# Row stores before a weight load, sums moved in the product sets, and the recurrence output rounded earlier

## What is computed

```python
x = rms_norm(x + expert_layer(...), final_g)          # end of the first block
mod = silu(c) @ w_mod + b_mod                          # shift, scale, gate
h = rms_norm_2(x, g_pre) * (1 + scale) + shift
q, k, v, g_att, u, g_lru, merge = split(h @ w_in)      # all products of h
y_a = (dilated_attention(q, k, v) * silu(g_att)) @ w_pa
u = causal_depthwise_conv(u, conv_w, conv_b)
y_b = (rg_lru(u, ...) * silu(g_lru)) @ w_pb            # the recurrence
gate_a, gate_b = split(sigmoid(merge))
out = (gate_a * y_a + gate_b * y_b) @ w_o
return x + gate * rms_norm_2(out, g_post)
```

## Time and profile before

| | us |
|---|---|
| median of 3 runs | 2854.6 |
| lowest and highest | 2853.25, 2855.59 |
| the profiled execution | 2852.03 |
| its span, first to last instruction | 2850.2 |
| mean granted TensorE clock | 0.988 of full |
| PE busy | 2767.2 (97%) |
| DVE, ACT, POOL busy | 1935.3, 1527.7, 213.5 |

### The profile page before, as it was taken

One profiled execution on the slowest core, in us unless ns is written; L12 is line 12 of the kernel. 1 busy time (PEld: TensorE's weight loads), 2 busy tenths in 40 slices (PEclk: granted clock), 3 DMA queues, 4 the chain that ended last, 5 costly groups with the idle time before them and its releaser, 6 DMA issues.

```text
span 2850.2 us, 33686 instructions
## 1 busy us (share of the span) xinstructions
PE 2767.2 (97%) x13612; PEld 2320.9 (81%) x13612; DVE 1935.3 (68%) x2215; ACT 1527.7 (54%) x1671; POOL 213.5 (7%) x129
## 2 busy tenths in 40 slices
PE   8999999889999999999999988999999999997999
PEld 7889988678888888888888866888888888886887
DVE  8563467778888888888888886554434442665654
ACT  5322322257777777777777765233444344995122
POOL 0211000100000000000000003321000000110000
PEclk9999999989999999999999998999999999999999
DMA  6222157789999999999999941333222221113542
GB/s 199 88 78 74 70 179 269 279 335 386 383 389 382 382 389 386 385 387 382 385 384 381 377 159 68 111 110 134 67 60 68 81 78 59 48 47 130 167 155 89
DMA packets 153276, 611.57 MB, mean 215 GB/s; under 512 B 26784, under 2 KB 52768, under 8 KB 96672
## 3 DMA queue, kind: packets, MB, share of 16 engines
q1 hardware_dynamic: 148224, 592.68, 55.8%
q0 software_dynamic: 4464, 16.25, 2.2%
q10 hardware_dynamic: 432, 0.47, 0.1%
HBM read 549.35 MB, written 58.82 MB: 213 GB/s over the span
## 4 chain that ended last, share of the span: by engine, by line
PE 89%; DVE 5%; ACT 2%; DMA 2%; issue 1%; POOL 1%; SPq 0%; POOLq 0%; DVEq 0%; ACTq 0%
PE bank L463 23%; PE bank L465 23%; PE bank L464 23%; PE bank L1892 12%; PE bank L471 3%; DMA b_raw<-in_w_sets_dram 1%; PE bank L2722 1%; DVE b_pl L2372 1%; POOL b_sum L2350 1%; PE bank L799 1%; PE bank L1441 0%; PE bank L480 0%; ACT b_ph L2364 0%; PE bank L3149 0%; ACT b_sy L2415 0%
## 5 line engine op out<-in xcount | busy, mean ns | idle before, releaser
L1840 DVE TENSOR_TENSOR e_wl<-e_raw,e_wh 128x2048 fp32r<-128x2048 f32 x381 | 870.9, 2291 | 123.8 <-ACT e_wh L1832 123.3
L1832 ACT ACTIVATE e_wh<-e_raw 128x2048 fp32r<-128x2048 f32 x384 | 735.5, 1919 | 184.6 <-PE bank L465 101.0
L463 PE MATMUL bank<-e_wh,e_xh 128*128 128x512 f32 x1020 | 403.5, 396 | 0.0
L465 PE MATMUL bank<-e_wh,e_xl 128*128 128x512 f32 x1020 | 398.3, 390 | 0.0
L464 PE MATMUL bank<-e_wl,e_xh 128*128 128x512 f32 x1020 | 397.0, 389 | 0.0
L463 PE MATMUL bank<-b_hid_h,b_wh 128*128 128x512 f32 x828 | 327.2, 395 | 4.1 <-DVE b_hid_l L2224 3.4
L465 PE MATMUL bank<-b_hid_h,b_wl 128*128 128x512 f32 x828 | 323.3, 390 | 0.0
L464 PE MATMUL bank<-b_hid_l,b_wh 128*128 128x512 f32 x828 | 323.1, 390 | 0.0
L465 PEld LDWEIGHTS bank<-e_wh,e_xl 128*128 128x128 f32 x1020 | 191.5, 188 | 40.9
L464 PEld LDWEIGHTS bank<-e_wl,e_xh 128*128 128x128 f32 x1020 | 191.8, 188 | 38.1
L463 PEld LDWEIGHTS bank<-e_wh,e_xh 128*128 128x128 f32 x1020 | 191.6, 188 | 37.9 <-DVE e_wl L1840 0.4
(11 more groups left out here) (566 smaller groups left out, 5029.0 us busy)
## 6 DMA issues: line engine op xcount, KB each, us to landing
e_raw<-in_e_gate_dram SPq DMA_DIRECT2D x128, 1024.0 KB, 7.4
e_raw<-in_e_up_dram SPq DMA_DIRECT2D x128, 1024.0 KB, 7.5
e_raw<-in_e_down_dram SPq DMA_DIRECT2D x128, 1024.0 KB, 7.8
b_raw<-in_w_dram SPq DMA_DIRECT2D x26, 1024.0 KB, 5.5
a_raw<-in_w_dram SPq DMA_DIRECT2D x12, 1024.0 KB, 5.7
a_mod_w<-in_w_mod_dram SPq DMA_DIRECT2D x48, 256.0 KB, 5.0
b_raw<-in_w_sets_dram SPq DMA_DIRECT2D x10, 1024.0 KB, 5.2
a_x<-in_x_dram SPq DMA_DIRECT2D x16, 512.0 KB, 5.2
```

The costliest lines, as they stand in the source:

```text
L463: e.matmul(out, a[0], b[0], start=first, stop=False)
L465: return e.matmul(out, a[1], b[0], start=False, stop=last)
L1832: e.activation(t.e_wh[s][:, 0:2048], t.e_raw[slot][:, 0:2048], ACT.Copy).then_inc(*e.inc("e_round", i))
L1840: e.tensor_tensor(t.e_wl[s][:, 0:2048], t.e_raw[slot][:, 0:2048], t.e_wh[s][:, 0:2048].bitcast(F32), ALU.subtract).then_inc(*e.inc("e_spli ...
```

## The change

Four things are altered.

1. SP stores `b_t` 0 to 3 before it waits for `w_split` 0 and loads set 0. `b_c` 1 moves from `b_t` 4 to 7 to a place behind them, so the second half waits for `b_gained` 7 and not for its stores; ACT's `early` of values 2 and 3 moves into the second turn.
2. The weight sums get other buffers. POOL makes the four sums of set 0 before it crosses the quarters of h, as soon as the last rows are placed (`placed` 7), and no longer after `crossed_low` 3. The crossed quarters and the results `set_y` get other places.
3. Every set takes its products in another order: rows, rows, rows, then the four crossed ones. The first two need no weight sum, the first three no crossed quarter. The results are put together in other steps: product 2 is added last, within the step of product 5, and sigmoids are done at steps 1, 5 (two) and 6 in place of 3, 4, 5 and 6. ACT and DVE round parts 0 to 2 before the crossed quarters.
4. `p_lh` 2 to 7 moves off `b_hid`, so the recurrence output is rounded in slots 1, 2 and 4, its low parts 0 to 3 by POOL and 4 to 7 by DVE in slot 4. `m_ba` moves onto `b_hid` and waits for the last merge product. `a_in` becomes two buffers; the first two weight pieces are loaded in slot 0, the heads in slot 3.

The arithmetic is the same but for the order of some additions. The diff, cut:

```diff
+        places = {1: (10240, 4096), 4: (14336, 6144), 2: (18432, 20480), 3: (8192, 12288)}
+        self.set_sum = [sb(f"b_sum{i}", y + at, [128, 4, 128]) for i, at in enumerate((16384, 17920, 16896, 17408))]
-        self.m_ba = (sb("m_bah", y + 8192, [128, 4, 1024], F32R), sb("m_bal", y + 12288, [128, 4, 1024], F32R))
+        self.m_ba = (sb("m_bah", hid, [128, 4, 1024], F32R), sb("m_bal", hid + 4096, [128, 4, 1024], F32R))
-        self.a_in = sb("m_a", y + 16384, [128, 12, 130])
+        self.a_in = [sb(f"m_a{i}", y + at, [128, 12, 130]) for i, at in enumerate((16384, 14400))]
-        self.p_lh = [sb(f"p_lh{i}", (raw if i < 2 else hid) + 1024 * i, [128, 1024], F32R) for i in range(8)]
+        self.p_lh = [sb(f"p_lh{i}", raw + 1024 * i if i < 2 else y + 6144 + 1024 * i, [128, 1024], F32R) for i in range(8)]
-        self.o_w = (sb("o_wh", hid, [128, 8, 1024], F32R), sb("o_wl", y, [128, 8, 1024], F32R))
+        self.o_w = (sb("o_wh", y + 8192, [128, 8, 1024], F32R), sb("o_wl", y, [128, 8, 1024], F32R))
...
 
 def act_turn_second(e, t, half, behind):
     cols = slice(512 * half, 512 * half + 512)
-    e.wait_ge(*e.at(f"b_t_out{half}", 4 * half + 3))
+    e.wait_ge(*(e.at("b_gained", 7) if half else e.at("b_t_out0", 3)))
...
@@ -2263,14 +2263,13 @@
 def act_round_crossed(e, t, n):
     for j in range(4):
         e.wait_ge(*e.at("crossed_pool" if n in (1, 4) else "crossed", n, j))
-    e.wait_ge(*e.at("b_turned", 1, 7))
+    e.wait_ge(*{1: e.at("b_t_out1", 7), 2: e.at("b_turned", 0, 7), 3: e.at("b_t_out1", 7),
+                4: e.at("crossed_low", 2)}[n])
     e.activation(t.mix_cols[n][0][:, :, :], crossed_cols(t, n), ACT.Copy).then_inc(*e.inc("crossed_high", n))
...
-SUM_OF = {3: 0, 1: 1, 2: 2, 5: 3}
-
-
-SET_OUT = {3: (3, 1, 1), 4: (0, 0, 0), 5: (1, 0, 1), 6: (2, 1, 0)}
+SUM_OF = {5: 0, 3: 1, 4: 2, 2: 3}
+
+
+SET_OUT = {1: (3, 0, 0), 2: (0, 0, 1), 5: (2, 1, 1), 6: (1, 1, 0)}
+
+
+SET_DONE = {1: (1,), 5: (5, 2), 6: (6,)}
...
@@ -2337,16 +2339,17 @@
 
     a, s = set_quarters(t, g), [x[:, :, :] for x in t.set_sum]
     e.wait_ge(*e.at(f"raw{g % 2}_in", "set", g))
-    for k, (i, x, y, how) in enumerate(((3, a[1][0], a[1][1], ALU.add), (1, s[0], a[0][0], ALU.subtract),
-                                        (2, a[0][0], a[1][0], ALU.subtract), (5, a[0][1], s[1], ALU.subtract))):
+    for k, i, x, y, how in ((0, 5, a[1][0], a[1][1], ALU.add), (1, 3, s[0], a[0][0], ALU.subtract),
+                            (3, 2, a[0][1], s[1], ALU.subtract), (2, 4, a[0][0], a[1][0], ALU.subtract)):
         if g == 0:
-            e.wait_ge(*e.at("crossed_low", 3))
+            e.wait_ge(*e.at("placed", 7, 1))
+            e.wait_ge(*e.at("e_y_out", N_EXPERTS - 2))
         else:
             e.wait_ge(*e.at("part_low", 7 * (g - 1) + i))
-        if i == 1:
+        if i == 3:
+            e.wait_ge(*e.at("set_sum", g, 5))
+        if i == 2:
             e.wait_ge(*e.at("set_sum", g, 3))
-        if i == 5:
-            e.wait_ge(*e.at("set_sum", g, 1))
         e.tensor_tensor(s[k], x, y, how).then_inc(*e.inc("set_sum", g, i))
...
-    for i, x in enumerate((rows(0, 0), cross(2), cross(3), cross(1), rows(1, 0), rows(1, 1), cross(4))):
+    for i, x in enumerate((rows(0, 0), rows(1, 0), rows(1, 1), cross(2), cross(3), cross(1), cross(4))):
         q, b = 7 * g + i, set_bank(g, i)
-        if g == 0 and i in (1, 2, 3, 6):
-            e.wait_ge(*e.at("crossed_low", {1: 2, 2: 3, 3: 1, 6: 4}[i]))
+        if g == 0 and i >= 3:
+            e.wait_ge(*e.at("crossed_low", (2, 3, 1, 4)[i - 3]))
...
+    if kind == "merge":
+        for out in SET_DONE.get(i, ()):
+            y = t.set_y[SET_OUT[out][0]][s]
+            e.wait_ge(*e.at("set_taken", g, out))
+            e.activation(y[:, :], y[:, :], ACT.Sigmoid).then_inc(*e.inc("set_sig", g, out))
+            e.mark("set_made", g, out)
...
 def dve_set(e, t, g, i):
+    b, b2 = set_bank(g, i), set_bank(g, 2)
+    bank, bank2 = bank_by(t, b, r), bank_by(t, b2, r)
+    def made(out):
+        if kind == "values":
+            e.mark("set_made", g, out)
+    if i not in (0, 2):
+        set_out_free(e, g, 1)
+        e.tensor_tensor(fourth, bank, first, ALU.add).then_inc(*e.evict(b, "set_taken", g, 1))
+        made(1)
+    if i == 3:
+        e.wait_ge(*e.at("set_one", g))
+        e.tensor_tensor(first, bank, first, ALU.add).then_inc(*e.evict(b, "set_begun", g, 3))
+    if i == 4:
+        e.wait_ge(*e.at("set_begun", g, 3))
+        set_out_free(e, g, 6)
+        e.tensor_tensor(second, bank, first, ALU.add).then_inc(*e.evict(b, "set_begun", g, 4))
+    if i == 5:
+        e.wait_ge(*e.at("set_begun", g, 4))
+        e.tensor_tensor(third, bank, second, ALU.add).then_inc(*e.inc("set_taken", g, 5))
+        made(5)
+        e.tensor_tensor(first, bank, first, ALU.add).then_inc(*e.evict(b, "set_begun", g, 5))
+        e.wait_ge(*e.at("set_full", g, 2))
+        e.wait_ge(*e.at("set_begun", g, 5))
+        e.tensor_tensor(first, bank2, first, ALU.add).then_inc(*e.evict(b2, "set_taken", g, 2))
+        made(2)
+        e.wait_ge(*e.at("set_begun", g, 4))
+        e.tensor_tensor(second, bank, second, ALU.add).then_inc(*e.evict(b, "set_taken", g, 6))
+        made(6)
...
-    for i in range(8):
+def sp_store_t(e, t, half):
+    for i in range(4 * half, 4 * half + 4):
...
     act_scale(e, t, 1)
-    early(2, 0)
-    early(3, 0)
-    act_turn_second(e, t, 1, lambda kk: None)
+    def behind_second(kk):
+        if kk in (1, 3):
+            early(2 + kk // 2, 0)
+
+    act_turn_second(e, t, 1, behind_second)
     e.activation(t.stat[:, 3, :], t.stat[:, 2, :], ACT.Sqrt).then_inc(*e.inc("r1_root"))
-    act_round_crossed(e, t, 1)
-    act_round_crossed(e, t, 3)
-    act_round_crossed(e, t, 2)
     early(0, 1)
     early(1, 1)
-    act_round_crossed(e, t, 4)
...
-    for q in range(4):
+    for q in range(3):
         act_round_part(e, t, q)
+    act_round_crossed(e, t, 2)
+    act_round_crossed(e, t, 3)
+    act_round_part(e, t, 3)
+    act_round_crossed(e, t, 1)
     early(2, 1)
     early(3, 1)
+    act_round_crossed(e, t, 4)
...
-    for n in (1, 3, 2):
-        dve_low_crossed(e, t, n)
-    for q in range(2):
+    for q in range(3):
         dve_low_part(e, t, q)
+    dve_low_crossed(e, t, 2)
+    dve_low_crossed(e, t, 3)
+    dve_low_part(e, t, 3)
+    dve_low_crossed(e, t, 1)
     dve_low_crossed(e, t, 4)
-    for q in range(2, AHEAD):
+    for q in range(4, AHEAD):
         dve_low_part(e, t, q)
     st = t.stat
...
 def pool_second(e, t):
+    pool_set_sums(e, t, 0)
     for j in range(4):
         pool_cross(e, t, 1, j)
     for j in range(4):
         pool_cross(e, t, 4, j)
-    for g in range(N_SETS):
+    for g in range(1, N_SETS):
         pool_set_sums(e, t, g)
 
 
 def sp_second(e, t):
+    sp_store_t(e, t, 0)
     sp_load_set(e, t, 0)
-    sp_store_t(e, t)
+    sp_store_t(e, t, 1)
 
...
     for kk in range(8):
-        if piece_of_lru(kk) == slot:
+        if LRU_SLOTS[kk] == slot:
             act_round_lru(e, t, kk)
...
         e.wait_ge(*e.at("gated2", i))
+        e.wait_ge(*e.at("merge", N_MERGES - 1))
         e.activation(t.m_ba[0][:, :, 128 * i:128 * i + 128], t.g_in[i % 2][:, :, :],
...
             dve_low_piece(e, t, i)
-    for kk in range(8):
-        if piece_of_lru(kk) == slot:
-            dve_low_lru(e, t, kk)
+    for kk in range(4, 8):
+        if slot == 4:
+            low_lru(e, t, kk, "lru_low")
...
+    for kk in range(4):
+        low_lru(e, t, kk, "lru_low_pool")
...
         e.dma_start(t.sig2[6 + slot // 4, half, which], t.m_sig[n][:, :]).then_inc(*e.dma(f"m_sig_out{n}", slot))
-        if slot == 1:
-            sp_load_heads(e, t, 0)
+        if slot == 0:
             sp_load_piece(e, t, 0)
             sp_load_piece(e, t, 1)
+        if slot == 3:
+            sp_load_heads(e, t, 0)
+            sp_load_mix_gate(e, t, 0)
+            sp_load_heads(e, t, 1)
         sp_mix_steps(e, t, slot)
...
-            e.wait_ge(*e.at("mixed", i - 1))
-        e.dma_start(t.a_in[:, :, :], t.scr_heads[rows]).then_inc(*e.dma("a_in", i))
+        if i >= 2:
+            e.wait_ge(*e.at("mixed", i - 2))
+        e.dma_start(t.a_in[i % 2][:, :, :], t.scr_heads[rows]).then_inc(*e.dma(f"a_in{i % 2}", i))
...
+        sp_load_mix_gate(e, t, MIXES[slot] + 1)
+        sp_load_heads(e, t, MIXES[slot] + 2)
...
+LRU_SLOTS = (1, 1, 2, 2, 2, 4, 4, 4)
...
+def lru_high_free(e, kk):
+
+    e.wait_ge(*e.at("lru_made", kk))
     if kk < 2:
         e.wait_ge(*e.at("w_split", MERGE_TILE))
+    elif kk < 5:
+        e.wait_ge(*e.at("conv_made", 7))
+        e.wait_ge(*e.at("lru_made", 6))
     else:
-        e.wait_ge(*e.at("merge", N_MERGES - 1))
+        lru_over(e)
...
+def low_lru(e, t, kk, name):
     e.wait_ge(*e.at("p_lh", kk))
     e.tensor_tensor(t.p_ll[kk][:, :], t.lru[:, kk, :], t.p_lh[kk][:, :].bitcast(F32),
-                    ALU.subtract).then_inc(*e.inc("p_l", kk))
+                    ALU.subtract).then_inc(*e.inc(name, kk))
+    e.mark("p_l", kk)
```

(46 more changed lines are left out.)

49 lines of the change are left out of this document (20 added, 29 removed).

## The result

| | before | after |
|---|---|---|
| median of four runs (range), us | 2854.61 (2853.25 to 2855.59) | 2811.71 (2809.95 to 2812.62) |
| profiled execution: time, span, us | 2852.03, 2850.2 | 2809.95, 2807.7 |
| PE busy, us | 2767.2 | 2758.6 |
| mean granted clock | 0.988 | 0.993 |

The ratio is 0.9849 (95% interval 0.9832 to 0.9866): 42.1 us less between the two profiled executions, where the forecast's sum had 40.6. First the page of after, beside the earlier trace rows; then PE's waits, beside the earlier trace rows (waited for, total us, times, longest us).

What follows compares the result with a forecast made beforehand. PE, busy 97% of the span, bounds the kernel, with 33.5 us of reachable waits and slow clock behind. Terms 14.0 - 2.5 + 5.5 + 6.4 + 0.5 + 16.7 = 40.6 us give 2811.4 profiled, median 2814.0, range 2807.5 to 2823.

Steps and rivals of the forecast that it cites:

- Stores, 14.0: Before the first value products: 12.1 us wait for `b_hid` high, 1.6 of clock and a 0.3 wait go, 14.0 us gained.
- Sums on POOL, -2.5: POOL's set 0 sums beside DVE's path to the second turn: two collisions of 1.55, less 0.6 cover, 2.5 us lost.
- The main case: On DVE's path to the second turn, POOL holds only large two-input operations, 2.5 us lost; chance 0.45.
- The rival: POOL's lock holds DVE's small operations on `stat` too: second turn 3.9 us late, 6.3 lost with clock, 2817.8; chance 0.20.
- it is short enough to leave the clock alone: PE's wait from POOL's sums, at the second turn, lowers no clock: 2.2 us did no harm before, 3.4 did.
- Second half, 5.5: Second half of the value products: the 3.4 us wait for `b_hid` low and 2.1 of clock go, 5.5 us gained.
- Order of products, 6.4 and 0.5: At set 0 the 3.6 us wait for `b_pl` and slow clock go, 6.4 us; behind the sets 0.5 us gained.
- the slower loop: In the sets, three chained DVE additions lengthen the loop; past a period of 20.6 us PE waits; chance 0.02.
- Recurrence output, 16.7: Behind the merge products: waits of 1.2 us (`m_mix`) and 12.7 (`p_ll`) and 2.8 of clock go, 16.7 us gained.
- the rival of that run: One-buffer run: the second token tile's mixing comes 4 to 5 us late, PE waits 2 to 5 us, 2814 to 2820.

Runs made afterwards that it cites:

- the experiment: Changed kernel, product order kept, but ACT and DVE round crossed parts 2, 3 and 1 ahead of set 0's parts: 2815.96 us, ratio 0.9869.
- the three: Late rounding, all low parts on DVE and one buffer for the heads; all put into the changed kernel together: 2818.89 us, ratio 0.9877.
- both kernels with the old tail: The kernel before (2854.61 us), and the kernel before with only the stores of rows 0 to 3 moved ahead of set 0's load (2837.81 us).

## Why the prediction was right, and where it was not

- **Stores, 14.0:** right. The chain's last link went; three stores, now alone, landed in 2.6 us (median), where the last took 9.0. The edit alone moved the second turn by 13.8 us, and undoing it cost 13.9. In the changed kernel 0.4 us of the wait for `b_hid` high stayed, where the forecast had none, and the stretch behind gave 1.4 us; counted from L480 the part is some 13.5.
- **Sums on POOL, -2.5:** the size was right (2.4), the mechanism half. The main case took two collisions of large operations; in fact there was one large (0.98), a brush with the gain (0.16), and two with small operations (0.96 and 0.98). That two times 1.55 and this sum both come to 3.1 is luck. The rival had the rule right and priced each of its three collisions at 1.5, where they cost 1.0. The step "it is short enough to leave the clock alone" fell: in half of the profiles it did not. That `l_wgl`'s 2.2 us did no harm, on which the step rested, is true of both kernels that have this wait, and of the 2.2 us for `m_mix` with one buffer; it did not carry over to the second turn.
- **Second half, 5.5:** right, 5.3 when undone (3.4 of waiting).
- **Order of products, 6.4 and 0.5:** right in kind, 5.4 in the experiment. The landmarks give 3.5 us behind the first set product, where the forecast had 3.3 (2.8 and 0.5). Merge-set loads come every (1934.98 - 1856.69) / 4 = 19.6 us, not 20.0, against 20.7 before: the head tile's load is earlier still, and the slower loop did not come.

```profile
1856.69 0.43 SPq L2335 DMA_DIRECT2D b_raw<-in_w_sets_dram  x1
...
1934.98 0.43 SPq L2134 DMA_DIRECT2D b_raw<-in_w_dram  x1
```

- **Recurrence output, 16.7:** the sum was right (15.6 behind the first `p_lh` product, and the 1.2 for `m_mix`), the cause only in part. It laid the late roundings to the rounding slots and to the mixing's single buffer. One buffer alone costs 2.4 us (`m_mix` 2.2), the rival of that run, and 0.9 us (237.8 - 236.9) when the rounding is late too; some 7 us of the 15.6 lie outside the three, by the traces in SP's order. That the sum came out is partly luck: the change moved these loads too, but the forecast had no term for it. It followed SP's order for the stores and not for the two loads in slot 1, though ACT's 9.7 us of idle time stood in the trace of before.
- **Not in the sum:** the 2.2 us for `l_wgl`. With 0.3 us more they make the 2.5 by which the stretch between the sets and the first `p_lh` product beat the forecast; 0.7 us were missing up to there, 0.5 of them lost ahead of L480, so that the landmarks end 1.9 us ahead of it. Without this wait the forecast would have been met to 0.3 us, closer than the terms for POOL and the recurrence deserve.

## What to carry to other kernels

When work goes to POOL, list every DVE operation that it can meet, the shortest too: on a serial path each costs up to one POOL operation, and a wait on the new work that lets the path pass first is free as long as its result is wanted later. Behind a late instruction look one engine further back, for an idle time of that engine's own whose releaser is a DMA, and then at what its load stood behind in its queue. Compare two traces by the starts of the same PE instructions: the differences add up, and a gain that nobody forecast shows at once.

## What the runs showed of the hardware

*The same short wait lowered the clock in half of the profiles.* Five of ten showed a granted clock of 0.57 to 0.62 over the 4 us behind the same 2.2 to 2.4 us wait, five 1.00, and programs that are alike up to there stand on both sides. Each program was profiled once, so how often one and the same program falls is not shown.

*The operation of DVE or POOL that starts first holds the other up, and that can be worth more than the operations.* The last step of the recurrence, before (POOL, then DVE) and after:

```profile
2563.44 3.36 POOL L3387 TENSOR_TENSOR l_cvl<-l_cv,l_cvh 128x1024 fp32r<-128x1024 f32 x1 [20.10 <-ACT l_wgh L3272]
2566.76 2.50 POOL L3390 TENSOR_TENSOR l_wgl<-l_wg,l_wgh 128x128 fp32r<-128x128 f32 x1
```
```profile
2563.31 1.23 DVE L3189 TENSOR_TENSOR l_out<-l_t,l_gl 128x1024 f32<-128x1024 f32 x1
2564.99 3.96 DVE L2153 TENSOR_TENSOR b_wl<-b_raw,b_wh 128x2048 fp32r<-128x2048 f32 x1 [0.45 <-ACT b_wh L2147]
```
```profile
2539.82 2.40 POOL L3404 TENSOR_TENSOR l_cvl<-l_cv,l_cvh 128x1024 fp32r<-128x1024 f32 x1 [19.78 <-ACT l_cvh L3285]
2542.18 1.45 POOL L3407 TENSOR_TENSOR l_wgl<-l_wg,l_wgh 128x128 fp32r<-128x128 f32 x1
```
```profile
2540.00 3.30 DVE L3204 TENSOR_TENSOR l_out<-l_t,l_gl 128x1024 f32<-128x1024 f32 x1
```

Before, DVE's product began 0.13 us ahead of POOL's low part; POOL waited for it, then `l_wgl` waited for DVE's next, long operation, and PE for `l_wgl`. After, POOL began 0.18 us ahead and PE waited for nothing. That the order makes the wait is read from the traces and was not tried by an edit. It was no accident of one run: both kernels with the old tail show 3.35 to 3.36 and 2.50 us and the wait of 2.2, all those with the changed one 2.40 to 2.42 and 1.44 to 1.46. The code of the step is the same. Why POOL started there some 0.3 us later behind its input before is not settled; that it has no work behind that pair is not the reason, since the wait stays away with all low parts on DVE.
